# Expert weights of a mixture-of-experts block: `w_down` in 2 MB blocks with a 16 KB row for each partition

## The reference

```python
gu = xb @ w_gate_up[e] + b_gate_up[e]          # w_gate_up[e]: 1024 x 2048
gate, up = gu[:, :D_EXPERT], gu[:, D_EXPERT:]
gate = jnp.minimum(gate, SWIGLU_LIMIT)
up = jnp.clip(up, -SWIGLU_LIMIT, SWIGLU_LIMIT)
glu = gate * jax.nn.sigmoid(SWIGLU_ALPHA * gate)
y = ((up + 1.0) * glu) @ w_down[e] + b_down[e]  # w_down[e]: 1024 x 1024
return y * wts[:, None].astype(y.dtype)
```

## Time and profile before

| | |
|---|---|
| median of three runs | 1282.21 us (1281.26 to 1282.87) |
| profiled execution, first to last instruction (its span) | 1279.8 us |
| median of the runs less that span | 2.4 us |
| PE busy | 1154.4 us, 90% |
| read from HBM | 463.79 MB, 363 GB/s over the span |
| granted TensorE clock, mean | 0.987 |

### The profile page before, as it was taken

One profiled execution on the slowest core, in us unless ns is written; L12 is line 12 of the kernel. 1 busy time (PEld: TensorE's weight loads), 2 busy tenths in 40 slices (PEclk: granted clock), 3 DMA queues, 4 the chain that ended last, 5 costly groups with the idle time before them and its releaser, 6 DMA issues.

```text
span 1279.8 us, 14568 instructions
## 1 busy us (share of the span) xinstructions
PE 1154.4 (90%) x5357; PEld 528.9 (41%) x5357; DVE 406.3 (32%) x905; ACT 154.1 (12%) x277; POOL 19.3 (2%) x24
## 2 busy tenths in 40 slices
PE   3999999995999999999999898989899999999994
PEld 0587688853333433323232333333232323232332
DVE  3467246537413312121313132131312121213133
ACT  1111123401000100000000000101000000000003
POOL 1000000002000000000000000000000000000000
PEclk9999999996999999999999999999999999999998
DMA  9987931174999899999999999999999999999991
GB/s 355 370 340 301 396 133 66 66 272 192 372 419 417 358 421 414 422 414 422 414 420 416 418 418 417 419 418 418 416 419 415 421 414 422 415 420 416 418 413 45
DMA packets 92211, 465.17 MB, mean 363 GB/s; under 512 B 8458, under 2 KB 9084, under 8 KB 56316
## 3 DMA queue, kind: packets, MB, share of 16 engines
q1 hardware_dynamic: 89000, 460.99, 88.9%
q10 hardware_dynamic: 2788, 2.82, 0.8%
q0 software_dynamic: 400, 1.05, 0.3%
HBM read 463.79 MB, written 1.05 MB: 363 GB/s over the span
## 4 chain that ended last, share of the span: by engine, by line
PE 42%; SPq 26%; DMA 22%; DVE 5%; issue 4%; ACT 1%; ACTq 0%; DVEq 0%
DMA arena<-in_w_down 21%; SPq L404 13%; PE ps L837 12%; SPq L410 11%; PE ps L601 8%; PE ps L855 6%; PE ps L724 2%; PE ps L747 2%; PE ps L817 2%; PE ps L825 2%; PE ps L696 2%; SPq L414 1%; PE ps L862 1%; PE ps L595 1%; PE ps L564 1%
## 5 line engine op out<-in xcount | busy, mean ns | idle before, releaser
L837 PE MATMUL ps<-arena 128*64 128x512 f32 x2048 | 448.7, 593 | 6.0 <-DMA arena<-in_w_gate_up 6.0
L837 PEld LDWEIGHTS ps<-arena 128*64 128x64 f32 x2048 | 146.1, 137 | 303.1 <-issue 278.8
L855 PE MATMUL ps<-arena 128*64 128x512 f32 x1024 | 234.1, 598 | 28.6 <-DMA arena<-in_w_down 28.0
L1464 DVE TENSOR_SCALAR arena<-ps 128x512 f32<-128x512 f32 x32 | 22.1, 691 | 484.8 <-PE ps L837 484.8
L855 PEld LDWEIGHTS ps<-arena 128*64 128x64 f32 x1024 | 69.0, 136 | 190.4 <-issue 139.7
L601 PE MATMUL ps<-arena 128*128 128x256 f32 x448 | 97.7, 379 | 0.0
L601 PEld LDWEIGHTS ps<-arena 128*128 128x128 f32 x448 | 84.9, 190 | 13.9 <-issue 2.6
L1090 ACT ACTIVATE arena<-arena 128x512 f32<-128x512 f32 x32 | 20.2, 630 | 569.8 <-DVE arena L1464 569.8
L1502 DVE COPY arena<-ps 128x512 f32<-128x512 f32 x34 | 23.5, 691 | 202.7 <-PE ps L817 202.7
L817 PE MATMUL ps<-arena 128*128 128x128 f32 x544 | 66.9, 283 | 22.5 <-ACT arena L1094 22.5
L817 PEld LDWEIGHTS ps<-arena 128*128 128x128 f32 x544 | 63.8, 196 | 26.6 <-issue 25.0
(11 more groups left out here) (245 smaller groups left out, 633.0 us busy)
## 6 DMA issues: line engine op xcount, KB each, us to landing
arena<-in_w_gate_up SPq DMA_DIRECT2D x256, 1024.0 KB, 20.0
arena<-in_w_down SPq DMA_DIRECT2D x128, 1024.0 KB, 15.6
arena<-in_w_ada SPq DMA_DIRECT2D x12, 2048.0 KB, 17.1
arena<-in_w_in SPq DMA_DIRECT2D x10, 2048.0 KB, 16.4
arena<-in_w_mix_out SPq DMA_DIRECT2D x2, 2048.0 KB, 9.2
arena<-in_w_hy_out SPq DMA_DIRECT2D x1, 2048.0 KB, 14.9
arena<-in_w_attn_out SPq DMA_DIRECT2D x1, 2048.0 KB, 19.8
arena<-in_x ACTq DMA_DIRECT2D x1, 1024.0 KB, 11.2
```

The lines of the kernel that those rows point to most:

```text
L837: last = mm(ps[64 * h:64 * h + 64, 4 + b, :], hTp[:, k, s * 64:(s + 1) * 64], w[:, b * 1024 + h * 512:b * 1024 + (h + 1) * 512], start=Fal ...
L855: last = mm(ps[64 * h:64 * h + 64, 6, :], lhs, slots[c][:, qq, h * 512:(h + 1) * 512], start=(q == 0), stop=(q == 7))
```

## The change

The host hands `w_down` over in another order, so that each 2 MB half of an expert's matrix is a block of 128 rows of 16 KB: row p of block c holds rows (4c + q) * 128 + p of the matrix for q = 0 to 3, one behind the other. The kernel moves such a block with one transfer. `w_down` goes in two transfers per expert in place of four; `dn_slot` is two slots of 2 MB, at the same place in SBUF; PE waits for a half and signals `dn_used` after a half; SP waits and issues by halves, for the last expert as well; ScalarE's count in `y_copy` follows. The matmuls and their order are the same. The reordering on the host is no part of the time.

```diff
-        dn_slot = [at("ring", 2048 * (KD + c), 2048).rearrange("p (q n) -> p q n", q=2) for c in range(4)]
-        last_down = [g.rearrange("p (q n) -> p q n", q=2) for g in gu_slot[:4]]
+        dn_row = [at("ring", 2048 * KD + 4096 * c, 4096) for c in range(2)]
+        dn_slot = [r.rearrange("p (q n) -> p q n", q=4) for r in dn_row]
+        last_down = [at("ring", 4096 * c, 4096).rearrange("p (q n) -> p q n", q=4) for c in range(2)]
...
-        s_dn = [sem(f"down_in{c}") for c in range(4)]
+        s_dn = [sem(f"down_in{c}") for c in range(2)]
...
             def down(c, item):
-                sp.dma_start(dn_slot[c], w_dn[0, item, c * 256:(c + 1) * 256, :].rearrange("(q p) n -> p q n", p=P))\
-                    .then_inc(s_dn[c], 16)
+                sp.dma_start(dn_row[c], w_dn[item, c]).then_inc(s_dn[c], 16)
...
-                for k in (2 * f, 2 * f + 1):
-                    gate_up(k, 0) if k < KD else down(k - KD, 0)
+                if 2 * f < KD:
+                    gate_up(2 * f, 0)
+                    gate_up(2 * f + 1, 0)
+                else:
+                    down(f - 4, 0)
...
             def stream_down(pair, expert, used):
-                for c in range(4):
-                    sp.wait_ge(S["dn_used"], pair * 8 + (used + c + 1))
-                    sp.dma_start(dn_slot[c], w_dn[0, bass.ds(expert, 1), c * 256:(c + 1) * 256, :]
-                                 .rearrange("o (q p) n -> p (o q) n", p=P)).then_inc(s_dn[c], 16)
+                for c in range(2):
+                    sp.wait_ge(S["dn_used"], pair * 4 + (used + c + 1))
+                    sp.dma_start(dn_row[c], w_dn[bass.ds(expert, 1), c].rearrange("o p n -> p (o n)"))\
+                        .then_inc(s_dn[c], 16)
...
-                stream_down(p, e_prev, -8)
+                stream_down(p, e_prev, -4)
                 stream(p, e_b, rest, True, 0)
-                stream_down(p, e_a, -4)
+                stream_down(p, e_a, -2)
...
-            for c in range(4):
-                sp.wait_ge(S["gu_used"], q * 16 + (16 + c + 1))
-                sp.dma_start(last_down[c], w_dn[0, bass.ds(e_b, 1), c * 256:(c + 1) * 256, :]
-                             .rearrange("o (q p) n -> p (o q) n", p=P)).then_inc(s_gu[c], 16)
+            for c in range(2):
+                sp.wait_ge(S["gu_used"], q * 16 + (16 + 2 * c + 2))
+                sp.dma_start(at("ring", 4096 * c, 4096), w_dn[bass.ds(e_b, 1), c].rearrange("o p n -> p (o n)"))\
+                    .then_inc(s_gu[c], 16)
...
             def down(landed, slots, count):
 
-                for c in range(4):
+                for c in range(2):
                     pe.wait_ge(landed[c], count)
-                    for qq in range(2):
-                        q = 2 * c + qq
+                    for qq in range(4):
+                        q = 4 * c + qq
...
-                act.wait_ge(S["dn_used"], i * 4 + 4)
+                act.wait_ge(S["dn_used"], i * 2 + 2)
...
+        if name == "w_down":
+            v = v[0].reshape(E, 2, 4, P, D).transpose(0, 1, 3, 2, 4).reshape(E, 2, P, 4 * D)
```

More of the change, by code:

```diff
@@ L419, in _ @@
             stream(1, 2, rest, False, -8)
-            stream_down(1, 1, -8)
+            stream_down(1, 1, -4)
             stream(1, 4, own, False, 0)
             stream(1, 3, rest, True, 0)
-            stream_down(1, 2, -4)
+            stream_down(1, 2, -2)
             sp.wait_ge(S["tables"], 2)
@@ L441, in _ @@
             stream(q, e_b, rest, True, 16)
-            stream_down(q, e_a, 4)
-            for c in range(4):
-                sp.wait_ge(S["gu_used"], q * 16 + (16 + c + 1))
-                sp.dma_start(last_down[c], w_dn[0, bass.ds(e_b, 1), c * 256:(c + 1) * 256, :]
-                             .rearrange("o (q p) n -> p (o q) n", p=P)).then_inc(s_gu[c], 16)
+            stream_down(q, e_a, 2)
+            for c in range(2):
+                sp.wait_ge(S["gu_used"], q * 16 + (16 + 2 * c + 2))
+                sp.dma_start(at("ring", 4096 * c, 4096), w_dn[bass.ds(e_b, 1), c].rearrange("o p n -> p (o n)"))\
+                    .then_inc(s_gu[c], 16)
             sp.wait_ge(S["gu_used"], q * 16 + 32)
@@ L1592 @@
     for name, value in list(inputs.items()) + list(host_tables().items()):
-        v = np.ascontiguousarray(value)
+        v = np.asarray(value)
+        if name == "w_down":
+            v = v[0].reshape(E, 2, 4, P, D).transpose(0, 1, 3, 2, 4).reshape(E, 2, P, 4 * D)
+        v = np.ascontiguousarray(v)
         arrays["in_" + name] = v
```

## The result

The changed kernel took 1273.4 us (median of 4 runs, 1272.9 to 1274.6) against 1282.5 for the kernel before in the same comparison: a ratio of 0.9924, 95% interval 0.991 to 0.9939. The forecast was 1274.3. The profiled execution's span went from 1279.8 to 1271.0.

A forecast was written before the change was run, and what follows sets the result against it. The DMA engines were taken to set the pace from about 490 to 1163 us. Longer rows (-9.6) and PE's later start (+1.7) took 1282.2 us to 1274.3, range 1272 to 1280.

The forecast's parts named there:

- The bound: From about 490 to 1163 us the DMA engines set the period, 60.25 us per pair of experts, PE 4.3 us ahead.
- Rows of 16 KB: `w_down` loads: 4.91 us per 2 MB half in place of 5.11, saving 9.6 us over 48 halves.
- the line: Time per MB against row count, through 2, 4 and 8 KB rows: 0.067 us per 128 rows, extended to 16 KB.
- PE's half at the end: At the last limited `down`, two quarters of matmuls follow the last landing instead of one: +1.72 us, once.
- Hand-over and cover: Refills requested by halves come up to 4.2 us later; 8.1 us of other queued transfers cover this, so no gap opens.
- the start of 2.3 us: Start-up time of a `w_down` transfer before its data flows, read from issues into an empty queue: 2.3 us.
- the two places that I named: Where late hand-over might open a DMA gap: first-half issues after the limited `down`, which waits for weights, and the free one.
- The signs: What would show it right: pair 59.45 us, 32768 fewer packets under 8 KB, `w_down`-only windows 427 GB/s, two PE waits.
- the missing wait at k = 7: PE's 0.55 us stall at the last k of `gate_up(p,0)`, before the limited `down`, was to disappear.
- The sum: Whole kernel: -9.6 for longer rows and +1.7 for PE's later start, -7.9 us in all.

The follow-up runs named there:

- the cut run: Changed kernel, but each 1 MB transfer reads contiguous 8 KB runs in HBM and writes them as separate 4 KB pieces in SBUF; 1283.3 us, ratio 1.0012 to before.
- run with `w_gate_up` too: Changed kernel with slices k and k + 1 of `w_gate_up` also moved as 2 MB transfers of 16 KB rows, with exceptions; 1267.5 us, 0.9893 of before.
- the whole hand-over: Changed kernel, but SP asks for both `w_down` halves only when PE has finished the whole `down`; 1299.4 us, 1.0134 of before.
- the one transfer: Changed kernel with one 4 MB `w_down` transfer per expert, 32 KB rows, wait and hand-over by the whole `down`; 1355.6 us, one run.

## Why the prediction was right

**The bound.** Right. The pair shrank by what the DMA engines saved, and PE still waits for landings in it: with 59.36 us it stays above the 55.99 of a pair without such waits.

**Rows of 16 KB.** The mechanism is shown: the time follows the number of pieces, not the transfers' number or size (4 KB rows in halves, 60.25), and not the layout in HBM (the cut run, 60.28). The term was mis-sized a little. Predicted were 0.80 us per pair and 9.6 in all; measured are 0.89, and 12 pairs at that are 10.7. The slope of the line was read too small. The kernel with 8 KB rows in quarters has that row length in all its 24 MB, so 59.65/24 = 2.486 us per MB is read there without any subtraction. With it the pair of before leaves (60.25 - 16 x 2.486)/8 = 2.560 for 4 KB rows, where 2.555 was read, and the changed kernel's 59.36 leaves 2.449 for 16 KB, where the line gave 2.454. The run with `w_gate_up` too has 22 MB of 16 KB rows in 58.89 us and gives 2.451. So 128 pieces less per MB save 0.074 us and not 0.067, 64 less save half of it, and for the 2 KB rows of `w_in` the same slope gives 387 GB/s, which is what the window shows. That is about 9 ns for each piece on its DMA engine (8 pieces per engine in 0.074 us). The rule of the Trainium skill, page "DMA: Bandwidth & Descriptors", section "Why small descriptors are slow (HBM only)", has the right form, a fixed cost for each packet, but an estimate by its 3 cycles is 4.2 us in all, and these runs show two and a half times that.

**PE's half at the end.** +1.72 predicted, +1.6 measured (118.5 against 116.9), and the two kernels that differ from before in one thing alone show it in the one with halves and not in the one with quarters.

**Hand-over and cover.** No gap opened, as predicted: the issues behind the limited `down` of the changed kernel land 10.8 to 10.9 us later. Of all the `w_down` issues between 520 and 1150 us none lands sooner than 10.8 us after it. But the cover was smaller than I counted: the start of 2.3 us was too short. 10.8 less 4.9 of data less the 3.0 us of start that the whole hand-over showed leave 2.9 us, not 4 (3.5 by the 2.4 of the one transfer). That run also shows the price past the cover, 2.1 us in the pair for 2.2 us of lateness. Of the two places that I named, only the one behind the limited `down` gives way in it.

**The signs.** The pair (59.36 against 59.45), the packets (but for 1024 small ones that I had not counted), the two waits (1.78 and 1.16 against 2 and 1.4) and the missing wait at k = 7 came as described. The windows with `w_down` alone, for which I had named 427 GB/s, say less than I had hoped. Five of them read from 410 to 440: over 7 or 8 us, a dozen rows of 16 KB per engine, one row more or less at the edge moves GB/s by several per cent.

**The sum.** -10.7 + 1.6 = -9.1 where -7.9 was predicted and the medians give -9.1. That the sum and the medians agree to the tenth is luck: the kernel before alone has medians from 1282.1 to 1283.8, and the two spans give -8.8. What was not foreseen at all is the clock: it did not matter here, where PE waits 1.8 us at most, but it did in the run with the late hand-over, where it waits 3 us in every pair.

## What to carry to other kernels

Where PE waits for landings and the DMA engines have no gap, count the pieces that a transfer is cut into on both sides, the row in HBM and the run in SBUF, and not the transfers: halving the pieces of a stream is worth here 3% of its time from 4 to 8 KB and 1.5% from 8 to 16, and from 16 to 32 nothing that could be read. Coarser hand-over is free only up to the cover, issue to landing less the transfer's own time less its start, and past that it cost here about a us for a us in every pair; so take the longer rows as far as slots can be handed over in time, and no further. A later start of the engine that waits is paid once, at the last wait, if it has slack in between.

## What the runs showed of the hardware

SP is blocked less by its issues when the transfers have fewer pieces. Before, issues of `w_down` blocked SP for up to 4.6 us with 26.6 us to landing at most; after, on all of them:

```profile
L413 SPq DMA_DIRECT2D arena<-in_w_down x60: 328/333/997, 357.3 to 1212.3; - x60
...
DMA to landing us min/median/max: 7.5/14.6/28.7
```

No issue of `w_down` in the pairs blocks for more than 1.0 us now, although up to 28.7 us pass to its landing. The other runs line up by the piece, not by the transfer. With pieces of 4 KB the longest such issue took 6.9 us (halves) and 4.8 us (1 MB, contiguous in HBM), with 8 KB 2.7 us (quarters) and 2.3 us (halves), and with 16 KB for `w_gate_up` as well 0.33 us, with 28.2 us to landing at most. That the queue is limited by pieces and not by bytes fits all of these; no run measures its depth.

PE's granted clock fell behind some waits for a landing and not behind others. Windows right behind the first wait of a limited `down`: one of the changed kernel (a wait of 1.78 us), three of the kernel with 4 KB rows in halves (2.35, 2.34 and 2.45 us), then two of the kernel with 8 KB rows in halves (2.01 and 1.75 us); the clock is the third number from the end:

```profile
791.50:794.00 2.50, 2.48 (x12) 1.07 (x14) 2.36 (x6) 0.00 (x0) 0.00 (x0) 1.00 1.00 426
```

```profile
738.20:740.70 2.50, 2.50 (x10) 1.10 (x12) 2.32 (x7) 0.00 (x0) 0.00 (x0) 0.74 1.04 415
798.40:800.90 2.50, 2.46 (x12) 1.09 (x14) 2.34 (x6) 0.00 (x0) 0.00 (x0) 1.00 1.02 408
858.70:861.20 2.50, 2.50 (x8) 0.88 (x10) 2.32 (x7) 0.00 (x0) 0.00 (x0) 0.53 1.03 411
```

```profile
792.60:795.10 2.50, 2.50 (x8) 0.94 (x10) 2.32 (x7) 0.00 (x0) 0.00 (x0) 0.67 1.02 426
852.30:854.80 2.50, 2.50 (x12) 1.01 (x14) 2.36 (x6) 0.00 (x0) 0.00 (x0) 1.00 1.01 419
```

Behind 1.8 us it stayed at full speed, behind 3.05 us it was at 0.62 to 0.64 in the three pairs read, and behind 7.9 us it was at 0.50 at once. In between the length of the wait alone does not decide: in the kernel with 8 KB rows in halves the `down` was drawn out (8.78 us) behind each of six waits of 1.98 to 2.04 us, while in the two kernels with 4 KB pieces and hand-over by halves many waits of 2.33 to 2.46 us had no such effect. What else decides stays open. In the 8 KB kernel the pairs alternate: a slowed `down` makes PE 0.26 us later, the next wait is 1.75 us, the clock stays, and the wait after that is 2.01 again.

In the kernels with halves the slower matmuls cost nothing, since PE then waits less later on (with 4 KB rows the pair is 60.25 all the same). With the later hand-over they delay the next request and are paid for.
